# Two stages in one block, paired index heads, a compact causal ring: one change to a hybrid two-block transformer kernel

## The reference, cut to what matters

```python
# second block, one layer (x2)
logits = einsum('bthd,bsd->bths', q_idx, k_idx) * HEAD_DIM ** -0.5      # 8 index heads, one key head
score  = einsum('bth,bths->bts', w_idx * 8 ** -0.5, relu(logits))       # causal, then top 256 of 1024 keys
sc     = einsum('bthd,btkd->bthk', q, k_sel) * attn_scale               # 8 heads, one key head, causal
out    = einsum('bthk,btkd->bthd', softmax(sc), v_sel)
y_a    = silu(z_a) * u * (spatial_mix(layer_norm(v)) + b_spatial)       # the "gating"
x      = layer_norm(ALPHA * x + gate * (concat(y_a, silu(z_b) * out) @ w_out))
```

## Time and profile before

| | us |
|---|---|
| median of 3 runs (lowest, highest) | 3168.41 (3166.29, 3173.77) |
| the profiled execution | 3164.96 |
| its span, first to last instruction | 3163.2 |

### The profile page before, as it was taken

One profiled execution on the slowest core, in us unless ns is written; L12 is line 12 of the kernel. 1 busy time (PEld: TensorE's weight loads), 2 busy tenths in 40 slices (PEclk: granted clock), 3 DMA queues, 4 the chain that ended last, 5 costly groups with the idle time before them and its releaser, 6 DMA issues. The chain is left out here.

```text
span 3163.2 us, 41488 instructions
## 1 busy us (share of the span) xinstructions
PE 2716.8 (86%) x13952; PEld 2125.2 (67%) x13952; DVE 2025.3 (64%) x4346; ACT 1578.6 (50%) x3061; POOL 1146.0 (36%) x981
## 2 busy tenths in 40 slices
PE   6999788698979997987989797996889697996887
PEld 5877566476868775665767585775667575774666
DVE  4372387597434624867974348897767358897756
ACT  3221276588422113756972216674864317674861
POOL 0100277464001003764630001985631001985631
PEclk9999899899989997998999898997999899997989
DMA  4443110100324421001013100110022100110022
GB/s 122 121 137 101 77 39 7 41 1 28 119 68 133 136 73 55 20 7 41 1 62 118 54 21 24 46 46 24 1 105 82 63 22 19 47 44 24 1 87 80
DMA packets 90754, 181.96 MB, mean 58 GB/s; under 512 B 12552, under 2 KB 27912, under 8 KB 90504
## 3 DMA queue, kind: packets, MB, share of 16 engines
q1 hardware_dynamic: 74124, 150.69, 14.8%
q10 hardware_dynamic: 16416, 28.61, 3.0%
HBM read 149.87 MB, written 33.33 MB: 58 GB/s over the span
## 5 line engine op out<-in xcount | busy, mean ns | idle before, releaser
L681 PE MATMUL ps<-w_hi,hh 128*128 128x512 f32 (+1 forms) x640 | 241.1, 377 | 22.2 <-DVE w_lo L566 10.1
L1236 POOL TENSOR_SCALAR a_prob<-a_prob,a_ratio 128x1024 f32<-128x1024 f32 x64 | 71.9, 1124 | 506.7 <-DVE a_ratio L1195 506.7
L681 PE MATMUL ps<-w_hi,hl 128*128 128x512 f32 (+1 forms) x640 | 241.3, 377 | 0.0
L681 PE MATMUL ps<-w_lo,hh 128*128 128x512 f32 (+1 forms) x640 | 240.1, 375 | 0.0
L1658 PE MATMUL ps<-o_w_hi,hh 128*128 128x512 f32 x512 | 211.6, 413 | 32.2 <-DVE o_w_lo L1582 32.2
L2120 DVE TENSOR_SCALAR_CACHE_REDUCE select_rows<-masks,select_cuts 128x1024 bf16<-128x1024 int16 (+7 forms) x264 | 228.1, 867 | 0.2
L1658 PE MATMUL ps<-o_w_hi,hl 128*128 128x512 f32 x512 | 207.9, 406 | 0.0
L1658 PE MATMUL ps<-o_w_lo,hh 128*128 128x512 f32 x512 | 207.0, 404 | 0.0
L936 POOL TENSOR_SCALAR b_prob<-b_prob,b_recip 128x1024 f32<-128x1024 f32 x128 | 144.2, 1127 | 162.7 <-DVE b_recip L893 160.2
L1638 POOL TENSOR_TENSOR o_rstd<-o_rstd,nhalf 128x1 f32<-128x1 f32 x56 | 46.7, 833 | 422.5 <-DVE o_rstd L1519 243.2
L1184 DVE CUSTOM_DVE_ANT_0 a_prob<-ps,a_bias 128x1024 f32<-128x1024 f32 x128 | 151.6, 1221 | 58.9 <-PE ps L1321 58.9
(11 more groups left out here) (363 smaller groups left out, 8047.6 us busy)
## 6 DMA issues: line engine op xcount, KB each, us to landing
w_early<-in_w_in SPq DMA_DIRECT2D x108, 256.0 KB, 2.8
ada_w<-in_w_ada ACTq DMA_DIRECT2D x96, 256.0 KB, 2.7
w_raw<-in_w_in SPq DMA_DIRECT2D x84, 256.0 KB, 2.8
xcur<-aq SPq DMA_DIRECT2D x16, 512.0 KB, 4.0
y<-xcur SPq DMA_DIRECT2D x16, 512.0 KB, 3.7
a_bias<-bias_tiles SPq DMA_DIRECT2D x8, 960.0 KB, 4.8
bq<-in_w_out SPq DMA_DIRECT2D x12, 512.0 KB, 3.5
closing_rows<-in_w_out SPq DMA_DIRECT2D x12, 512.0 KB, 4.6
```

Of the source, the lines that this page charges most:

```text
L681: mm = nc.tensor.matmul(o, lhs, rhs, start=(k == 0 and i == 0), stop=(k == K - 1 and i == 2))
```

## The change

**Stages joined.** `heads_phase` leaves its block open and returns a `Seam` (its phase and five counts); `closing_phase` puts its programs into the same block. The new waits are SP and ACT on the last output product (`pv_done`), ACT on the gates (`mixed`), ACT before chunk 1 on the last y (`y_done`), PE before its first product on the last output read (`o_read`). The semaphores of both stages are cleared together in the next block.

**Compact ring, gates later.** The causal ring has slots of the lengths that their rows have; nothing is lent, and DVE's wait before row 12 is gone. The eight gates come at g = 18, 22, ... 46, after that row's predecessor has been scaled.

**Index heads in pairs.** One staging tile for the keys; queries are transposed in pairs of heads straight from `q_idx`, so five rounds instead of ten. ACT copies both banks (with the scale) as the high part, DVE subtracts for the low part. Scores are made for two heads at a time: six matmuls of 64 rows for each 512 keys, where two heads had four of 128 rows. The relu ring has three rows instead of two; PSUM holds two pairs instead of four heads.

```diff
 class Phase:
-    def __init__(self, nc):
+    def __init__(self, nc, joins=None, continued=False):
...
             def _(sp):
-            for s in Phase.stale:
-                sp.sem_clear(s)
+            if not self.joins:
+                for s in Phase.stale:
+                    sp.sem_clear(s)
             program(sp)
 # heads_phase
-        pr = sb("prob", [P, RING - len(lent), S])
+        pr = sb("prob", [P, ring_at(RING)])
...
-                    elif g == RING - len(lent):
-                        dve.wait_ge(mixed, len(gating))
...
-                        if g <= len(gating):
-                            gate(g - 1)
                         b = g - 1
                         pool.wait_ge(recip, b + 1)
                         nc.gpsimd.tensor_scalar(prob(b), prob(b), rr[:, b % NS:b % NS + 1], 0.5, ALU.mult,
                                                 ALU.mult).then_inc(normed, 1)
+                    if g >= 18 and g % 4 == 2 and (g - 18) // 4 < len(gating):
+                        gate((g - 18) // 4)
                     n = (g - READ) // QB
                     if (g - READ) % QB == 0 and 0 <= n < NSB:
                         close(n)
 # closing_phase
-        with Phase(nc) as ph:
+        with Phase(nc, joins=seam.ph) as ph:
 # SP
+                sp.wait_ge(seam.pv_done, seam.products)
 # ACT
+                act.wait_ge(seam.pv_done, seam.products)
+                act.wait_ge(seam.mixed, seam.gates)
                 for k in range(K):
...
+                    if k == 1:
+                        act.wait_ge(seam.y_done, 4 * seam.pairs)
                     nc.scalar.activation(by_tile(hh[:, k, :]), source(k), ACT.Copy).then_inc(src_hi, 1)
 # PE
+                pe.wait_ge(seam.o_read, 8 * seam.pairs)
 # index_phase: ACT, DVE, PE
+                for z in range(NP + 1):
+                    act.wait_ge(turned, z + 1)
+                    nc.scalar.activation(stack(z, 0), turned_pair(z), ACT.Copy, scale=scale_of(z)).then_inc(ev_act, 1)
...
+                for z in range(NP + 1):
+                    dve.wait_ge(ev_act, z + 1)
+                    nc.vector.scalar_tensor_tensor(stack(z, 1), turned_pair(z), scale_of(z), stack(z, 0).bitcast(F32),
+                                                   ALU.mult, ALU.subtract).then_inc(ev_dve, 1)
...
+                pe.wait_ge(ev_dve, NP + 1)
+                for u, (qb, p) in enumerate(units):
+                    if u >= 2:
+                        pe.wait_ge(relued, 2 * (u - 1))
...
-                        nc.tensor.matmul(o, lhs, k_st[:, 0, k0:k0 + w], start=True, stop=False)
-                        mm = nc.tensor.matmul(o, lhs, k_st[:, 1, k0:k0 + w], start=False, stop=True)
+                        for i, (qe, ke) in enumerate([(0, 0), (0, 1), (1, 0)]):
+                            for m in range(2):
+                                half = slice(m * HD, (m + 1) * HD)
+                                mm = nc.tensor.matmul(ps[:, 4 * (u % 2) + 2 * m + k0 // BANK, 0:w],
+                                                      stack(p + 1, qe)[half, tok], stack(0, ke)[half, k0:k0 + w],
+                                                      start=(i == 0), stop=(i == 2))
```

More of the change, by code:

```diff
@@ L90, in __exit__, with __init__ @@
             Phase.stale = self.sems
+class Seam:
+    def __init__(self, ph, pv_done, products, o_read, y_done, pairs, mixed, gates):
+        self.ph, self.pv_done, self.products, self.o_read = ph, pv_done, products, o_read
+        self.y_done, self.pairs, self.mixed, self.gates = y_done, pairs, mixed, gates
 def clear_stale(nc):
@@ L682, in _, with heads_phase @@
                         mm.then_inc(bank_done, 1)
-def heads_phase(nc, env, tag, groups, queries, group_of, y_of, bias=None, load=(), ahead=(), lent=(), gating=()):
+def heads_phase(nc, env, tag, groups, queries, group_of, y_of, bias=None, load=(), ahead=(), gating=()):
     causal = bias is not None
@@ L717, in keys, with ring_at @@
         return (query_tile(g) + 1) * P if causal else S
+    def ring_at(slot):
+        return sum(keys(g) for g in range(slot))
     def tiles(n):
@@ L1349, in _, with closing_phase @@
                         turn(e)
-def closing_phase(nc, a, env, source, w_out, x_from, x_to, hh, hl, late, free, post, following, opened, early, mod):
+def closing_phase(nc, a, env, source, w_out, x_from, x_to, hh, hl, late, free, post, following, opened, early, mod, seam):
     ps, ident = env["ps"], env["ident"]
@@ new lines, in _ @@
+                nc.scalar.activation(stg.rearrange("p t (two d) -> p t two d", two=2),
+                                     k_idx[:, :, 0:HD].unsqueeze(2).broadcast_to([P, T, 2, HD]), ACT.Copy).then_inc(staged, 1)
+                for z in range(NP + 1):
+                    act.wait_ge(turned, z + 1)
+                    nc.scalar.activation(stack(z, 0), turned_pair(z), ACT.Copy, scale=scale_of(z)).then_inc(ev_act, 1)
+                for i, (qb, h) in enumerate(rows):
+                    n = (qb + 1) * P
+                    act.wait_ge(sc_done, i // 2 + 1)
+                    if i >= RL:
+                        act.wait_ge(summed, i - RL + 1)
+                    bank = 4 * (i // 2 % 2) + 2 * (i % 2)
+                    nc.scalar.activation(rl[:, i % RL, 0:n],
+                                         ps[:, bank:bank + 2, :].rearrange("p b n -> p (b n)")[:, 0:n],
@@ L2388, in _ @@
                                         ALU.mult).then_inc(scaled, 1)
[L2389 to L2400, removed]
+                for z in range(NP + 1):
+                    dve.wait_ge(ev_act, z + 1)
+                    nc.vector.scalar_tensor_tensor(stack(z, 1), turned_pair(z), scale_of(z), stack(z, 0).bitcast(F32),
+                                                   ALU.mult, ALU.subtract).then_inc(ev_dve, 1)
                 dve.wait_ge(scaled, 1)
-                for u, (qb, h) in enumerate(units):
+                for u, (qb, h) in enumerate(rows):
                     n = (qb + 1) * P
@@ L2494, in second_layer @@
                       following=None if last else (cols[:, 1, :], cols[:, 0, :], True),
-                      opened=[(tile, sem) for tile, _, sem in opening], early=early, mod=None if last else l + 1)
+                      opened=[(tile, sem) for tile, _, sem in opening], early=early, mod=None if last else l + 1, seam=seam)
     return following, hh, hl, early
```

107 lines of the change are left out of this document (40 added, 67 removed).

## The result

| | before | after |
|---|---|---|
| median (lowest to highest), us | 3167.35 (3163.41 to 3173.77), 4 runs | 3135.83 (3127.96 to 3137.64), 4 runs |
| ratio after/before | | 0.9894, 95% interval 0.987 to 0.9917 |
| profiled execution, us | 3164.96 | 3137.64 |
| its span, us | 3163.2 | 3135.6 |

A second set of executions on another chip gave 3132.0 against 3165.41, ratio 0.9902 (0.9887 to 0.9917). The forecast was 3140.2 with 3124 to 3157. The two profiled spans differ by 27.6 us; the sum forecast 28.2.

A forecast was written before the change was run, and what follows sets the result against it. Bounds: DVE in the index loop, an engine-to-engine chain in sparse attention; PE idles at the boundary. From 3164.96: -16.6 (staging, loop), -6.0 (sparse attention), -6.8 (boundary), +1.2 (semaphores), +3.45 (median) gives 3140.2 us, range 3124 to 3157.

The forecast's parts named there:

- Index staging: Transposes ahead of the first index score, five rounds instead of ten: 6.4 us gained per layer, between 5.0 and 7.2.
- Index loop: Index score loop, DVE waiting less for ACT's relu with three ring rows: 1.9 us gained per layer, between 0 and 2.0.
- rival of half clock in the loop: Index score loop: 64-row score matmuls at 1.2 GHz lose 8.5 us per layer against the forecast, 3157 us; chance 0.08.
- Start of sparse attention: First rows without gates between them: PE's 7.77 us wait gone, DVE's split 0.8 faster; 8.6 us gained per layer, 3 to 8.6.
- The start isn't freed: Start of sparse attention: another latency takes PE's 7.77 us, 3 us gained instead of 8.6, 3151 us; chance 0.13.
- Later gates: Later in sparse attention: gates ahead of critical rows at g = 22, 30, 38, 46 lose 5.6 us per layer, 0 to 21.
- POOL becomes the bound: Sparse attention, g = 18 to 46: POOL's queue never empties, sixteen gates cost 58 us, kernel slower at 3187; chance 0.06.
- Gates hidden: Sparse attention: later gates cost nothing; together with a free port at the boundary 3123.0 us; joint chance 0.14.
- Boundary: Heads to closing, four times: ACT 3.2 us earlier, less 1.5 for POOL and DVE colliding; 1.7 gained each, 6.8 in all.
- Port free: Heads to closing: the boundary gives 3.2 us; together with later gates costing nothing 3123.0 us; joint chance 0.14.
- Semaphores: End of kernel: 21 more semaphore clears behind the last DMA lose 1.2 us; behind the other three closings nothing.
- 3.45 us added for the median: Whole kernel: the median of the runs lay 3.45 us above the profiled execution, so this was added to the sum.

The follow-up runs named there:

- the ring of two: The changed kernel with a relu ring of two rows instead of three: 3143.86 us, 0.9925 of the kernel before.
- the late y: The changed kernel with POOL's last output sum and product behind DVE's fourth closing subtract, ACT's y wait at chunk 3: 3132.38 us, 0.9902 of the kernel before.
- two blocks: The changed kernel with heads and closing in separate blocks again, the seam's five waits gone: 3141.55 us, 0.9927 of the kernel before.

## Why the prediction was right, and where it was not

- **Index staging.** Right in its working: from the first transposes to the first add 18.0 us became 10.6 in the first layer and 17.9 became 11.4 in the second, 7.4 and 6.4 gained for 6.4. The first lies just outside the bound of 7.2: there the first eight transposes took 1.17 us, not 1.84. DVE's five operations took 1.23 us each, for 1.28, and waited for PE and ACT ahead of the second and third round, as assumed. The kernel with the old stage confirms staging and loop together: 18 to 19 us for 16.6.
- **Index loop.** 1.6 and 1.5 us gained for 1.9, and the ring of two gives just these back. The rival of half clock in the loop was half true: the granted clock fell from 0.96 to 0.92, but PE is busy 31.9 of 47.6 us and DVE doesn't wait for it.
- **Start of sparse attention.** The wait went, and nothing took its place. The term was too small: block 0 is read 10.2 us earlier in both layers, for 8.6. The missing piece is the clock: in the kernel before PE ran at half clock from the 2nd us, through the pause of 7.8 us, to the 25th (to the 28th in the second layer); now it does so to the 13th. *The start isn't freed* falls.
- **Later gates.** The four places were right and the waits nearly so, 6.2 us of them for 5.6; in eleven of the sixteen layers with these gates they are 7.2 to 7.5, since two of them reach 3.1. But the cost is some 8 us per layer by the means above, 8.8 in the first layer and 4.9 in the second between the changed kernel and the one without gates (154.3 against 145.4, 154.6 against 149.7), and by the timed ratios 4 to 5 against that kernel and 6 to 7 against the gates one row later. This is the term that was too small: a wait of PE was priced at its length, and the lower clock of that stretch at nothing. *POOL becomes the bound* had such a term, 1.0 us for each stall at half clock, but for sixteen of them; there are eight. *Gates hidden* falls here, for this placement.
- **Their sum was luck.** The forecast of 3.0 us per layer stands beside a trace that shows 2.9 and 3.8. But the kernel with early gates and compact ring says that the move itself brings at most 1 us per layer: block 15 at 155.6 and 155.2 against 154.3 and 154.6 in the changed kernel's first profile, 156.0 and 154.1 in its second. The other 2 to 3 us are stretches at half clock that the profile of the kernel before had (0.95 between the blocks, against 0.99 with early gates) and others have at other blocks. That the compact ring has a part in them is neither shown nor excluded.
- **Boundary.** 2.0 us per boundary for 1.7: the collision cost 1.22 us and not 1.5, and the late y shows that it is POOL's. The Trainium skill, SBUF — State Buffer, section Who interferes with whom, has the later of two such instructions blocked until the first has ended; the trace agrees, POOL's multiply ending 1.13 us behind DVE's first subtract, and DVE's second 1.08 behind that multiply. *Port free* falls. The half clock behind the boundary was left at "the same moment or sooner": 14, 8, 7 and 7 products for 12, 12, 10 and 12, so it went either way.
- **Semaphores.** 1.3 us at the end for 1.2. All of it lies behind the issue of the last DMA, where the clears stand (7.3 us to the end of the span for 6.0), and it is gone with two blocks. That the clears take it, and not something else at the end of a joined block, is likely and was not tried by itself.
- **The 3.45 us added for the median** were no property of the kernel: the next profiled execution lay 1.8 above its median.

## What to carry to other kernels

Work on a side engine costs by its place in that engine's queue ahead of the item that the bound engine wants next, and not by its amount: the same eight gates cost some 8 us per layer or 0.3 to 0.4 us one row apart. Read each queue for the critical item and put such work right behind it. Look at the granted clock of the stretch in which a new wait of TensorE falls, since such a wait can cost more than its length, and don't take a sum that comes out right as proof of its terms.

## What was not expected of the hardware

- The granted clock was lower in stretches with recurring short waits: 0.90 to 0.92 between block 0 and block 15 with four waits of 0.6 to 3.1 us for POOL, 0.93 to 0.99 without them. The half clock doesn't simply follow these waits. In the first sparse layer of the changed kernel it stands in the four stretches below. The second begins 1.1 us behind the wait of 2.09 us, the last 0.5 us ahead of the wait of 2.93; the first and third begin 1.8 and 1.2 us behind waits of 1.4 us for DVE that kernels without late gates have too. So what sets it off stays open.

```profile
2224.00:2230.80 6.80, 6.49 (x31) 4.54 (x27) 3.60 (x9) 4.10 (x10) 6.18 (x7) 0.50 0.00 0
2237.70:2241.10 3.40, 3.40 (x19) 2.96 (x18) 2.05 (x6) 3.25 (x8) 1.55 (x3) 0.50 0.02 5
2261.70:2265.00 3.30, 3.30 (x18) 2.63 (x15) 1.19 (x4) 0.99 (x4) 3.00 (x3) 0.50 0.03 7
2271.90:2278.60 6.70, 3.77 (x20) 3.16 (x19) 2.24 (x10) 2.72 (x9) 4.64 (x5) 0.50 0.00 0
```

- The same sparse stage of the same program differs by 2 us in the changed kernel, and by 4.3 us between the layers of the kernel without gates, where the granted clock is 0.99 in one and 0.93 in the other.
- Transposes of the identity, 0.113 us each, held the clock at 1.00 through a pause of 6 us; 22 of them, ending 3.7 us ahead of the next product, did not. The Trainium skill, TensorE: Matmul & The Clock Gate, section What's actually happening, has an engine idle for some time fall to half rate; these two runs agree with it.
- How long the half clock lasts behind the same pause of 6.1 us differed from 3.1 to 6.2 us.
